# A two-layer kernel: token halves in the last four chunks, the order of two softmax steps, and where later operands start

## What is computed

```python
o = gate0 * softmax(q kc + bias) vc + gate1 * softmax(q ks + bias) vs + gate2 * softmax(q kw + bias) vw
h = x + o @ w_out
x = rmsnorm(h + (silu(a) * b) @ w_down)
merged = sigmoid(g_a) * (y_a @ w_proj_mlstm) + sigmoid(g_b) * (y_b @ w_proj_pool)
out = x + rmsnorm(merged @ w_out_2)
```

## Time and profile before

| | us |
|---|---|
| median of 3 runs (lowest, highest) | 2150.17 (2149.57, 2150.26) |
| the profiled execution's own time | 2150.19 |
| its span | 2148.5 |
| PE, PE's weight loads, DVE, ACT, POOL busy | 2132.1, 1868.8, 1413.5, 1048.7, 62.7 |

### The profile page before, as it was taken

How to read it: one execution, slowest core, us unless ns; L and a number is a source line. 1 busy time by engine, 2 the same in 40 slices (tenths; PEclk the granted TensorE clock), 3 DMA queues, 4 the chain that set the end, 5 groups by cost and what they waited for, 6 DMA issues and landing times.

```text
span 2148.5 us, 34224 instructions
## 1 busy us (share of the span) xinstructions
PE 2132.1 (99%) x12178; PEld 1868.8 (87%) x12178; DVE 1413.5 (66%) x1913; ACT 1048.7 (49%) x1371; POOL 62.7 (3%) x114
## 2 busy tenths in 40 slices
PE   9999999999999999999999999999999999999998
PEld 8888889888888888888888888888888888888886
DVE  7767766766666666645556767867777676566564
ACT  6565665554444444444445555444454454444443
POOL 1001221000000000000000000000000000000000
PEclk9999999999999999999999999999999999999999
DMA  8585334556555565555555455545555555555553
GB/s 301 184 278 187 121 129 138 186 177 200 190 176 200 180 197 185 186 186 196 185 186 182 168 170 193 183 160 187 186 181 176 172 186 185 190 190 187 185 198 138
DMA packets 109317, 396.58 MB, mean 185 GB/s; under 512 B 12386, under 2 KB 12402, under 8 KB 109104
## 3 DMA queue, kind: packets, MB, share of 16 engines
q1 hardware_dynamic: 106848, 386.97, 53.3%
q0 software_dynamic: 2240, 8.38, 1.2%
q10 hardware_dynamic: 144, 0.03, 0.0%
HBM read 390.87 MB, written 2.13 MB: 183 GB/s over the span
## 4 chain that ended last, share of the span: by engine, by line
PE 95%; ACT 2%; DVE 2%; issue 1%; POOL 0%; DMA 0%; POOLq 0%; DVEq 0%; SPq 0%; ACTq 0%
PE set L1569 49%; PE set L1577 25%; PE set L1595 4%; PE set L1601 2%; PE set L1539 2%; PE set L1541 2%; PE set L1540 2%; ACT prob L588 1%; PE misc L1785 1%; PE misc L1712 1%; PE set L1683 1%; PE set L1525 1%; PE set L1526 1%; PE set L1527 1%; DVE prob L1050 0%
## 5 line engine op out<-in xcount | busy, mean ns | idle before, releaser
L815 DVE TENSOR_TENSOR w_hl<-raw,w_hl 128x1024 fp32r<-128x1024 f32 x729 | 884.3, 1223 | 560.9 <-ACT w_hl L491 554.8
L491 ACT ACTIVATE w_hl<-raw 128x1024 fp32r<-128x1024 f32 x729 | 762.1, 1056 | 790.9 <-PE set L1577 356.0
L1569 PE MATMUL set<-x_hl,w_hl 128*128 128x512 f32 x3520 | 857.3, 393 | 0.0
L1569 PEld LDWEIGHTS set<-x_hl,w_hl 128*128 128x128 f32 x3520 | 644.5, 188 | 124.4 <-issue 0.7
L1577 PEld LDWEIGHTS set<-x_hl,w_hl 128*128 128x128 f32 x3520 | 452.8, 191 | 18.3 <-issue 0.7
L1577 PE MATMUL set<-x_hl,w_hl 128*128 128x256 f32 x3520 | 462.6, 283 | 0.0
L1569 PE MATMUL set<-f_hl,w_hl 128*128 128x512 f32 x704 | 171.6, 395 | 0.0
L1569 PEld LDWEIGHTS set<-f_hl,w_hl 128*128 128x128 f32 x704 | 129.3, 188 | 27.1
L498 ACT ACTIVATE cross<-set 128x512 f32<-128x512 f32 (+1 forms) x142 | 83.1, 585 | 123.4 <-PE set L1569 111.1
L1577 PEld LDWEIGHTS set<-f_hl,w_hl 128*128 128x128 f32 x704 | 90.2, 188 | 4.3
L1595 PE MATMUL set<-w_hl,x_hl 128*128 128x512 f32 x384 | 92.9, 391 | 0.0
(11 more groups left out here) (324 smaller groups left out, 1789.1 us busy)
## 6 DMA issues: line engine op xcount, KB each, us to landing
raw<-in_weights SPq DMA_DIRECT2D x730, 512.0 KB, 4.1
bias_g<-bias POOLq DMA_DIRECT2D x4, 572.0 KB, 3.6
cur<-in_cur POOLq DMA_DIRECT2D x4, 535.0 KB, 3.5
h<-in_x SPq DMA_DIRECT2D x4, 512.0 KB, 7.4
bias<-u_dram POOLq DMA_DIRECT2D x1, 2048.0 KB, 13.4
out<-y_t SPq DMA_DIRECT2D x8, 256.0 KB, 2.4
post_row<-in_post POOLq DMA_DIRECT2D x1, 1024.0 KB, 7.7
w<-in_w POOLq DMA_DIRECT2D x1, 256.0 KB, 4.8
```

The lines of the kernel that those rows point to most:

```text
L491: a(high, whole, ACT.Copy).then_inc(hi_ready, 1)
L815: tt(low, whole, high.bitcast(F32), ALU.subtract).then_inc(lo_ready, 1)
L1569: last = mm(out[:, f * 2 * S:(f + 1) * 2 * S], w[:, 0, c], hl[:, kt, :, :], start=first and k == 0, stop=low_first, skip_group_check=True)
```

## The change

Three edits. (1) The last four chunks run their t = 0 halves in a row and then their t = 1 halves; all four `w_hl` slots stay in use until then. `half_out` comes after the fourth t = 0 half, `chunks_done` counts up in the t = 1 halves. At the end `square_out(3, 1)` moves behind the two `scale_out` of t = 0 on ACT, `finish(0, 1)` ahead of `post_variance(1)` on DVE, and SP stores t = 0 first. `splits` and its wait at L828 stay. (2) The four instructions of the compressed part come behind `mask_scores` in place of in front of it. (3) Three tensors that nothing uses shift what lies behind them: `o_hl` and its scope by 64 bytes, the scope of `f_hl` by 128 and the scope of `ya_hl`, `yb_hl`, `m_hl` (with the mLSTM's tensors) by 128.

```diff
+            o_lead = sb("o_lead", [P, 16], scope=s1c)
             o_hl = sb("o_hl", [P, HEADS, 2, S], F32R, scope=s1c)
...
+        f_lead = sb("f_lead", [P, 32], scope=s2)
         f_hl = sb("f_hl", [P, FKT, 2, S], F32R, scope=s2)
...
+        ya_lead = sb("ya_lead", [P, 32], scope=s3)
         ya_hl = sb("ya_hl", [P, KT, 2, S], F32R, scope=s3)
...
-        for t, q, ready, count in ((0, 0, y_ready, 1), (0, 1, y_ready, 2), (0, 2, y2_ready, 1), (1, 0, y_ready, 3),
-                                   (0, 3, y2_ready, 2), (1, 1, y_ready, 4), (1, 3, y2_ready, 3), (1, 2, y_ready, 5)):
+        for t, q, ready, count in ((0, 0, y_ready, 1), (0, 1, y_ready, 2), (0, 2, y2_ready, 1), (0, 3, y2_ready, 2),
+                                   (1, 0, y_ready, 3), (1, 1, y_ready, 4), (1, 2, y_ready, 5), (1, 3, y2_ready, 3)):
...
         square_out(3, 0)
         post_root(0)
-        square_out(3, 1)
...
         scale_out(0, 3)
+        square_out(3, 1)
         post_root(1)
...
                gate[:, bass.ds(head, 1), :, :].rearrange("p a b t -> p (a b) t"), ALU.mult).then_inc(share_ready, 1)
+        def make_parts(gi, n):
+            head = gi * HPG + n
             dve.wait_ge(share_ready, head + 1)
...
             if real(gi, n):
                 mask_scores(gi, n)
+            if real(gi, n - 1):
+                make_parts(gi, n - 1)
...
         finish(0, 0, m[0][:, :])
+        finish(0, 1, m[1][:, :])
         post_variance(1)
         dve.wait_ge(chunks_done, CHUNKS)
         take_out(3, 1)
-        finish(0, 1, m[1][:, :])
...
-        def block_tokens_apart(at, j, out, hl, kts):
+        def half_tokens(at, j, out, hl, kts, t, last_chunk):
...
-            for j in range(NB):
+            for j in range(NB if n < 3 else NB - RING):
...
+        for j in range(NB - RING, NB):
+            pe.wait_ge(lo_ready, at.at(j) + 1)
+            last = half_tokens(at, j, out, m_hl, (2 * j, 2 * j + 1), 0, j == NB - 1)
+        last.then_inc(half_out, 1)
+        for j in range(NB - RING, NB):
+            half_tokens(at, j, out, m_hl, (2 * j, 2 * j + 1), 1, j == NB - 1).then_inc(chunks_done, 1)
```

More of the change, by code:

```diff
@@ L1542, in block_tokens @@
             return last
-        def block_tokens_apart(at, j, out, hl, kts):
-            pe.wait_ge(lo_ready, at.at(j) + 1)
+        def half_tokens(at, j, out, hl, kts, t, last_chunk):
             w = w_hl[at.slot(j)]
[L1548 to L1557, removed]
+            for k, kt in enumerate(kts):
+                o = out[:, t * BLK:(t + 1) * BLK]
+                c = slice(k * BLK, (k + 1) * BLK)
+                x = slice(t * P, (t + 1) * P)
+                mm(o, hl[:, kt, 0, x], w[:, 0, c], start=False, stop=False, skip_group_check=True)
+                mm(o, hl[:, kt, 0, x], w[:, 1, c], start=False, stop=False, skip_group_check=True)
+                last = mm(o, hl[:, kt, 1, x], w[:, 0, c], start=False, stop=last_chunk, skip_group_check=True)
             return last
@@ L1998, in _ @@
             at, out = Pos(C_WO + n * NB), sets[(B_WO + n) % 2]
-            for j in range(NB):
+            for j in range(NB if n < 3 else NB - RING):
                 kts = (2 * j, 2 * j + 1)
                 wait = (m_ready, kts[1] // FT + 1) if n == 0 else None
[L2002 to L2005, removed]
+                chunk(at, j, wait, lambda: block_tokens(at, j, out, m_hl, kts, j == 0))
                 if n * NB + j in (3, 5, 7, 9):
                     rows_by_tokens((n * NB + j - 3) // 2)
+        for j in range(NB - RING, NB):
[4 more added lines that the diff above has]
+            half_tokens(at, j, out, m_hl, (2 * j, 2 * j + 1), 1, j == NB - 1).then_inc(chunks_done, 1)
     ctx.close()
```

## The result

The changed kernel takes 2136.10 us, the median of 4 runs (2136.04 to 2136.15), against 2149.87 for the kernel before on the same chip (4 runs, 2149.18 to 2150.26). The ratio is 0.9936, with a 95% interval of 0.9919 to 0.9953: the kernel is 0.6% faster. The forecast was 2137.3 us, between 2134 and 2142.

What follows compares the result with a forecast made beforehand. PE was taken to bound the kernel, busy 2132.1 of 2148.5 us. Attention, operand placement and the tail gave 2150.19 - 7.7 - 4.0 - 1.2 = 2137.3 us, range 2134 to 2142.

Steps and rivals of the forecast that it cites:

- attention: Attention heads: with the mask ahead of the compressed part, waits of 8.2 us go, 0.5 is charged back; gain 7.7 us.
- `m_hl`: Chunks by tokens with `m_hl`: laid like the weights' slots, twelve matmuls take 0.06 us less, 1.9 us in all.
- `o_hl`: `o_hl` chunks: moving it costs 0.1 us in units and 1.6 in `block_features`, 1.7 us together.
- `f_hl` and its like: Feature chunks with `f_hl`, `ya_hl`, `yb_hl`: laid like the weights' slots, 136 chunks gain 0.0285 us each, 3.8 us counted.
- the tail: Behind the last matmul: the time to the span's end falls from 8.9 to 7.7 us, a gain of 1.2 us.
- The waits of 8.2 us: Before the first matmul of `values`: 14 waits for the mask lose 0.40 to 0.85 us each; all should go.
- step c: Scores in six heads: DVE's block of q comes late for an earlier PE; 0.1 us charged each, 0.5 us together.
- step (d): Last head's wait on POOL: it moves along with the transposes before it, nothing gained or lost.
- the bound of 1.9: Tail: the gain would be 1.9 us, not 1.2, if DVE's wait for `chunks_done` didn't bind.
- A: Operand starts don't make the two rates, or unused tensors move nothing: placement gives 0, 2141.3 us; chance 0.13.
- B: A new wait at the scores or transposes takes half of attention's gain: 2141.1 us; chance 0.15.
- C: Operands that lie alike collide in PE's two reads: slower, 2159.7 us at 0.1 us a chunk; chance 0.02.

Runs made afterwards that it cites:

- part one alone: Only the compressed part's instructions moved behind `mask_scores`, on the kernel before: 2142.25 us against 2150.25, ratio 0.9963.
- the leads alone: Only the three unused tensors that shift later operands added, on the kernel before: 2144.07 us, ratio 0.9971.
- the three parts alone: The mask order, the unused tensors and the tail's edits, each by itself on the kernel before: 2142.25, 2144.07 and 2149.27 us.

## Why the prediction was right, and where its terms were off

The forecast time was 1.2 us too high. Two gains were larger than forecast and one cost smaller (attention, `m_hl`, `o_hl`, 1.7 together); two gains were smaller (`f_hl` and its like, the tail, 0.5).

**Attention, 7.7 forecast, 8.0 measured** (part one alone). The waits of 8.2 us went, as argued from the 1.04 us by which the mask moves. The 0.5 charged for six heads at the scores (step c) was not there: the scores show no idle time. All that is left is one late step at the first `values`, 0.2 us.

**`f_hl`, `ya_hl`, `yb_hl`, 3.8 forecast, 3.6 measured**, and **`m_hl`, 1.9 forecast, 2.3 measured.** The mechanism held; 0.06 us a dozen was read from starts with two digits, and over 281 steps the difference is 6.1 ns a matmul, 0.073 a dozen.

**`o_hl`, 1.7 forecast, 0.75 measured.** This is the step that failed most. The gross price was near the forecast (0.18 + 1.85), but the prediction hid only two chunks of it, and step (d) said that the last head's wait moves along with PE. For part one alone that is so: the wait stays at 1.5. It fails where the matmuls' rate changes, since the wait hangs on POOL beside DVE: slower matmuls shifted DVE's low part behind POOL's fourth multiplication, with part one and without it. That gave 1.28 back, for which the prediction had no term: the low net price is luck, though without it the total would still lie within the range.

**The tail, 1.2 forecast, 0.9 measured.** Each step of the sum was met within 0.1 us down to ACT's last scaling (2129.40, E + 3.0). POOL's addition was over earlier than forecast, at E + 4.3, but DVE's last `finish` beside it took 1.28 us and ended at E + 4.9, and the last two stores are issued one behind the other after it. So the end is 8.0 us behind E and not 7.7. That the wait for `chunks_done` binds was right, and taking it away shows its price: 0.45 to 0.49, where the bound of 1.9 put it at 0.7. Whether the last two stores in the other order would give more was not tried.

**The rivals.** A fell with the leads alone (-6.2 us) and for good with `x_hl` moved off (+6.1). B fell with the idle times. C, that operands which lie alike collide, fell for units by features, since 0 is quicker than 128. But 0 is not the best place: 64 is quicker by 0.024 us a chunk. Whether that is a collision was not shown.

Eight distances give rates from 2.760 to 2.828 us a chunk at one granted clock of 0.999. The Trainium skill's rule of two independent ports (SBUF — State Buffer, Who interferes with whom), from which the prediction read that the start of an operand is worth 0, is not borne out in that reading.

## What to carry to other kernels

Where PE is back to back, an operand's start against the loaded operand's, modulo 256 bytes, is worth testing: unused tensors gave this kernel 6 us with operands laid alike and 13 more with them 64 bytes apart; measure it for each form of matmul by itself. A wait that seems to move along with PE may be a collision of two other engines: look at whether the same instruction takes 0.6 or 1.6 us. When steps are put in a new order, look for old waits at the end of helpers, which now come later than what they guard.

## What was not expected of the hardware

- A matmul's pace depends on the distance of its two operands, by up to 2.5% a chunk (2.760 to 2.828 us), and differently for narrow, wide and loaded ones. Why is open: only starts were seen. The runs tell distance from place for a move of 128 bytes; for 32, 64, 96 and their like place and distance moved together.
- The best distance by features (64) is among the worst for 512 columns by tokens (234.2 ns against 227.9 at 0).
- POOL's 128x256 multiplication takes 0.61 us alone and 1.60 beside a low part of DVE that began 0.1 us earlier; one that began 0.2 us later itself takes 1.47 in place of 1.22.
- Costs did not add: the three parts alone give 15.2 us by their traces and 14.1 together, for `o_lead` gives 0.3 where heads still wait and costs 0.75 where they do not.
